# Hybrid decoder step: 32 sample tokens moved from the dense expert product to row gathers, gate values in two buffers

## The reference, cut to what matters

```
q  = standardize(x @ w_q)                 # 8 heads of 256
s1, s2 = scores of the two halves of q against 128 keys each
v1, i1 = top_k(s1, 16);  v2, i2 = top_k(s2, 16)
top_s, top_j = top_k(all 256 sums v1 + v2, 16)
expert = i1 * 128 + i2 of the chosen pairs   # one of 16384
gate   = softmax(top_s)
act = gelu(x . emb_u[expert]) * gate         # 8 x 16 = 128 experts a token
y   = sum of act * emb_v[expert]
```

## Time and profile before

| | us |
|---|---|
| median of 3 runs | 4821.25 |
| the profiled execution's own time | 4827.02 |
| its span, first to last instruction | 4825.2 |
| PE busy in the span | 4212.8 (87%) |
| DVE busy | 3123.2 (65%) |
| ACT busy | 1425.3 (30%) |
| POOL busy | 1019.4 (21%) |
| mean granted clock of PE | 0.938 of full |

### The profile page before, as it was taken

One profiled execution on the slowest core, in us unless ns is written; L12 is line 12 of the kernel. 1 busy time (PEld: TensorE's weight loads), 2 busy tenths in 40 slices (PEclk: granted clock), 3 DMA queues, 4 the chain that ended last, 5 costly groups with the idle time before them and its releaser, 6 DMA issues. The chain is left out here.

```text
span 4825.2 us, 61337 instructions
## 1 busy us (share of the span) xinstructions
PE 4212.8 (87%) x19753; PEld 3328.3 (69%) x19753; DVE 3123.2 (65%) x6997; ACT 1425.3 (30%) x2331; POOL 1019.4 (21%) x1145
## 2 busy tenths in 40 slices
PE   8999678667999999999588778898579999999995
PEld 1454334367999999999446522344569999999995
DVE  0144559996777777777545412489967777777776
ACT  0120013385323333332111100133672333333231
POOL 0000012294222222222100000112762222222221
PEclk9998799899999999999779988899899999999997
DMA  9777765535777777777377665655356777777773
GB/s 316 246 264 231 255 221 210 172 148 218 248 248 247 259 248 252 251 254 231 125 248 228 188 184 184 216 198 169 151 221 229 255 256 245 252 257 247 252 252 104
DMA packets 480396, 1083.53 MB, mean 225 GB/s; under 512 B 42782, under 2 KB 272175, under 8 KB 476672
## 3 DMA queue, kind: packets, MB, share of 16 engines
q1 hardware_dynamic: 289106, 680.98, 41.7%
q0 software_dynamic: 77392, 283.00, 18.0%
q10 hardware_dynamic: 113776, 118.10, 7.1%
HBM read 885.08 MB, written 196.83 MB: 224 GB/s over the span
## 5 line engine op out<-in xcount | busy, mean ns | idle before, releaser
L1494 PE MATMUL ps<-h_parts_d,u_parts_d 128*128 128x416 f32 x6144 | 1190.3, 353 | 26.6 <-ACT arena L1549 13.5
L1494 PEld LDWEIGHTS ps<-h_parts_d,u_parts_d 128*128 128x128 f32 x6144 | 1147.9, 188 | 59.0 <-ACT arena L1549 32.7
L1513 PE MATMUL ps<-a_parts_d,v_parts_d 128*128 128x416 f32 x4608 | 880.4, 351 | 4.3 <-DVE arena L1677 4.3
L1513 PEld LDWEIGHTS ps<-a_parts_d,v_parts_d 128*128 128x128 f32 x4608 | 861.3, 188 | 13.0 <-DVE arena L1677 5.7
L267 PE MATMUL ps<-ring,hT 128*128 128x512 f32 (+1 forms) x1440 | 637.2, 601 | 22.2 <-DMA ring<-in_gla_wo 12.1
L1544 ACT ACTIVATE v_parts_d<-ring 128x1024 fp32r<-128x1024 f32 x256 | 250.1, 1049 | 1034.6 <-PE ps L1513 1034.6
L1605 POOL DMA_INDIRECT arena<-in_peer_v,arena x256 | 240.9, 941 | 1432.6 <-DVE ps L1668 1430.2
L267 PEld LDWEIGHTS ps<-ring,hT 128*128 128x128 f32 (+1 forms) x1440 | 249.7, 177 | 379.4 <-issue 375.8
L1631 DVE TENSOR_TENSOR u_parts_d<-ring,u_parts_d 128x1024 fp32r<-128x1024 f32 x256 | 313.2, 1224 | 122.9 <-ACT u_parts_d L1542 122.9
L1605 POOL DMA_INDIRECT hT<-u_rows,arena x256 | 289.0, 1129 | 426.2 <-DVE hT L1652 375.0
L1542 ACT ACTIVATE u_parts_d<-ring 128x1024 fp32r<-128x1024 f32 x256 | 270.2, 1056 | 276.7 <-PE ps L1494 276.7
(11 more groups left out here) (269 smaller groups left out, 4380.7 us busy)
## 6 DMA issues: line engine op xcount, KB each, us to landing
ring<-in_peer_uT SPq DMA_DIRECT2D x256, 512.0 KB, 4.9
ring<-in_peer_v SPq DMA_DIRECT2D x256, 512.0 KB, 7.0
arena<-in_peer_uT SPq DMA_DIRECT2D x186, 512.0 KB, 5.5
u_rows<-arena SPq DMA_DIRECT2D x424, 128.0 KB, 4.0
gates_dense<-arena ACTq DMA_DIRECT2D x26, 2048.0 KB, 6.3
arena<-gates_dense ACTq DMA_DIRECT2D x64, 832.0 KB
ring<-in_ada_w SPq DMA_DIRECT2D x96, 512.0 KB, 4.7
u_rows<-arena SPq DMA_DIRECT2D x80, 512.0 KB, 6.3
```

The lines of the kernel that those rows point to most:

```text
L1494: mm = e.matmul(ps[:, tt % 2, 0:ND], w[:, m], hR[:, v, k], start=(k == 0 and n == 0), stop=(k == KC - 1 and n == 2))
L1513: mm = e.matmul(ps[:, 4 + m % 2, 0:ND], w[:, rows], aR[:, v, tt], start=begins, stop=ends)
```

## The change

The sample tokens leave the dense product: `ND` becomes 384. As 32 tokens of 128 experts each are as many rows as 128 partitions of 32, they are laid on all 128 partitions (four copies of the 32 tokens, two heads for each copy), and a turn gathers five rows (`ROWS`) where it gathered four. The fifth dot and the fifth accumulation stand at the end of `add_y`, the accumulation into `y_sample` in SBUF. In the search the sample tokens' queries of the four groups go to four quarters of one PSUM bank, behind the queries of each group's fourth tile, and are searched as one item: 17 items for 20. The gate table has 12 blocks. Two of the saved turns of `emb_u` go to the mixer's `stage_close`, four into the first four items of the search. The gates of a turn get two buffers, in the SBUF of `x`, which is kept in HBM meanwhile (`x_kept`) and loaded again behind the experts; the fifth rows of the gathers use it too. The loops of ACT and DVE hold two turns. ACT's `picked_gelu` stands later in its turn.

```
-DENSE = [(0, 0, 3 * P), (3 * P, SEQ, NS_TOK)]
-ND = 3 * P + NS_TOK
+ND = PICK * P
+ROWS = TPG + 1
+SPREAD = P // NS_TOK
-HEAD_TURNS, CLOSE_TURNS, IN_BUFS, OUT_BUFS = 70, 18, 2, 3
+HEAD_TURNS, CLOSE_TURNS, IN_BUFS, OUT_BUFS = 70, 20, 2, 3
...
# stage_close
-                    if w_o is not None and t < 4:
+                    if w_o is not None:
                         turner.turn(e, HEAD_TURNS + 2 * t + 10, HEAD_TURNS + 2 * t + 12)
...
+                if w_o is None:
+                    e.wait_ge(x_in, x_moved(l, 1))
...
-                        c = slice(DENSE[1][0], ND) if t > PICK else cols(t, np_)
+                        if t > PICK:
+                            for g in range(2):
+                                mm = e.matmul(ps[0:np_, 2 * (t % 4) + g, :], K["fold"], y_sample[:, g * 512:(g + 1) * 512], start=True, stop=True)
...
# stage_search
-            ITEMS = [(g, t, np_) for g in range(4) for t, np_ in TILES]
-            QBANKS = 3
-            turns_of = lambda n: range(VEC_TURNS + 2 * n, VEC_TURNS + 2 * n + 2)
+            ITEMS = [(g, t) for g in range(4) for t in range(4)] + [(3, 4)]
+            QBANKS, SAMPLE_BANK = 2, 2
+            turns_upto = lambda n: VEC_TURNS + 2 * n + min(n, 4)
+            turns_of = lambda n: range(turns_upto(n), turns_upto(n + 1))
...
                 def queries(n):
+                    g, t = ITEMS[n]
+                    if t > 3:
+                        return
                     if n >= QBANKS:
                         e.wait_ge(*qn_done(n - QBANKS + 1))
-                    q_rows.tile(e, n % NT, hT, n % QBANKS)
+                    q_rows.tile(e, t, hT, bank_of(n))
+                    if t == 3:
+                        q_rows.tile(e, 4, hT, SAMPLE_BANK, NS_TOK * g)
...
# stage_gates
-                body(NBLK // 2, 0)
...
+            def sp(e):
+                e.wait_ge(stage_over, 4 * here)
+                for i, np_ in TILES:
+                    e.dma_start(x_kept[i * P:i * P + np_], x[0:np_, i]).then_inc(x_in, 16)
...
# stage_experts
+            gt = [x.rearrange("p t c -> p (t c)")[:, v * DBLK * P:(v + 1) * DBLK * P].rearrange("p (b n) -> p b n", n=P) for v in range(2)]
+            u_got = [flat[:, j * D:(j + 1) * D] for j in range(TPG)] + [x[:, 3]]
+            v_got = [v_rows_buf[:, j] for j in range(TPG)] + [x[:, 4]]
...
# ACT, a turn
-                    if not first:
-                        picked_gelu(t - 1)
                     if not last:
                         e.wait_ge(*h_ps(t * TPG + 3))
                         hi_part(t + 1, 0)
...
                     a_hi(t, 2)
+                    if not first:
+                        picked_gelu(t - 1)
...
-                    if not last:
-                        gates(t + 1)
+                    if load:
+                        gates(t + 2, v)
...
# POOL, a turn
                     for j in range(TPG):
+                        if t:
+                            v_fetch(t - 1, j)
                     for j in range(TPG):
+                        u_fetch(t, j)
                     if t:
-                        v_fetch(t - 1)
-                    u_fetch(t)
+                        v_fetch(t - 1, TPG)
+                    u_fetch(t, TPG)
...
# DVE, add_y
+                    o = acc if j < TPG else y_sample
+                    e.scalar_tensor_tensor(out=o, in0=v_got[j], scalar=coef[:, j:j + 1], in1=o, op0=ALU.mult, op1=ALU.add
...
                         else:
                             dot(t, m - TPG)
+                    if not first:
+                        accumulate(t - 1, TPG)
+                    dot(t, TPG)
```

More of the change, by code:

```diff
@@ L257, in __init__, with tile @@
                 self.slots = {}
[L259 removed]
+            def tile(self, pe, t, src, bank, row=0):
                 np_ = TILES[t][1]
@@ L1587, in turn @@
                     a_hi(t, 3)
[L1588 to L1589 removed]
+                    if load:
+                        gates(t + 2, v)
                 e.sem_inc(h_read.sem, 2)
[L1592 to L1594 removed]
+                e.wait_ge(x_in, x_moved(l, 0))
+                gates(0, 0)
+                gates(1, 1)
+                o = spread.rearrange("p k (g n) -> p k g n", g=SPREAD)
+                e.activation(o, hT[:, :, SEQ:N].unsqueeze(2).broadcast_to([P, KC, SPREAD, NS_TOK]), ACT.Copy).then_inc(h_split.sem, 1)
+                e.activation(hR[:, 0], hT[:, :, 0:ND], ACT.Copy).then_inc(h_split.sem, 1)
                 hi_part(0, 0)
                 hi_part(0, 1)
[L1597 to L1600 removed]
+                turn(0, 0, first=True)
+                with e.Fori(0, turns // 2 - 2) as i:
+                    for u in (1, 2):
+                        turn(i * 2 + u, u % 2)
+                turn(turns - 3, 1)
+                turn(turns - 2, 0, load=False)
+                turn(turns - 1, 1, last=True, load=False)
                 picked_gelu(turns - 1)
@@ L1724, in dve @@
-                second_half(1)
-                with e.Fori(1, turns - 2) as t:
-                    first_half(t + 1)
-                    add_y(t)
-                    second_half(t + 1)
-                first_half(turns - 1)
+                for v in range(2):
+                    e.wait_ge(*xrow_ps(v + 1))
+                    b = 4 + 2 * v
+                    e.tensor_copy(xrow[:, v].rearrange("p (a k r) -> p k a r", a=4, k=KC),
+                                  ps[:, b:b + 2, :].rearrange("p b (k a r) -> p (b k) a r", a=4, r=STREAM)).then_inc(xrow_done.sem, 1)
@@ new lines, in dve @@
+                e.wait_ge(*xrow_done(2))
+                e.memset(Y[:, KEPT:].rearrange("p k n -> p (k n)"), 0.0).then_inc(zeroed.sem, 1)
+                e.memset(acc, 0.0).then_inc(zeroed.sem, 1)
+                e.memset(y_sample, 0.0).then_inc(zeroed.sem, 1)
+                e.wait_ge(*zeroed(3))
+                first_half(0, 0, 0)
+                second_half(0, 0)
+                first_half(1, 0, 1)
+                add_y(0, first=True)
+                second_half(1, 1)
+                with e.Fori(0, turns // 2 - 2) as i:
+                    for u in (1, 2):
+                        first_half(i * 2 + (u + 1), i + 1, (u + 1) % 2)
+                        add_y(i * 2 + u)
+                        second_half(i * 2 + (u + 1), (u + 1) % 2)
@@ L1730, in dve @@
+                first_half(turns - 2, turns // 2 - 1, 0)
+                add_y(turns - 3)
+                second_half(turns - 2, 0)
+                first_half(turns - 1, turns // 2 - 1, 1)
                 add_y(turns - 2)
-                second_half(turns - 1, last=True)
+                second_half(turns - 1, 1, last=True)
                 add_y(turns - 1)
@@ L1735, in dve @@
                 coefficients(turns - 1)
-                for j in range(TPG):
+                for j in range(ROWS):
                     accumulate(turns - 1, j)
```

344 lines of the change are left out of this document (175 added, 169 removed).

## The result

The changed kernel took 4863.36 us (median of 4 runs, 4856.74 to 4866.61) beside 4821.01 for the kernel before: a ratio of 1.0089, 95% interval 1.0071 to 1.0106. It is slower by 42 us where 54 less were forecast. Its profiled execution took 4860.7 us, with a span of 4858.9 and a mean granted clock of 0.915, where it was 0.938.

What follows compares the result with a forecast made beforehand. PE bounds the experts, DVE and PE nearly the search. Turns -15, gate buffers -6, experts' start and end +5, search -20, gates -24, mixers' close +6 sum to -54 us: 4767 us, range 4718 to 4810.

Steps and rivals of the forecast that it cites:

- Around the pause of 2.53 us in layer 0 it stayed at 1.00: Experts: PE's clock stayed at 2.4 GHz around one long pause in the earlier trace; used as evidence against rival B.
- rival B: Experts: the repeated pause makes PE's clock fall, 1.75 us in each of 62 turns, 4875 us; chance 8%.
- The pause: Experts: PE waits 2.7 us for the gelu in each turn instead of 0.24, from two added DVE instructions.
- The columns: Experts: 384 columns cost 174.5 ns a matmul for 187.8, 14.5 ns held fixed; 2.55 us less a turn.
- Rival C: Experts: the narrower matmul is no faster because weights set the pace; turn 38.2 us, 4882 us; chance 4%.
- Rival A: Experts: DVE's slack covers the added instructions, so a turn loses all of 2.55 us; 4629 us; chance 7%.
- Gates, gathers and gate buffers: Gates: one block fewer, -24 us; experts: nothing added for gathers, second gate buffer -6 us, both layers.
- The last pause of a layer: End of the experts: the last turn's pause of 2.53 us grows by 2.3 + 0.6 us.
- The search: Search: three items fewer for DVE, less PE losses: -10 us a layer, -20; from 0 to -37 a layer.
- the third turn of `emb_u`: Search, first four items: adds about 1.06 + 0.40 us each on PE; with the 6.3, some 10 us lost.
- Rival D: Search gains nothing or emb_u's third turn waits for loads, and turn gains nothing: 4802 us up; within forecast's range.
- The sample tokens' queries: Search: about 6.9 us more on PE once in four items, so DVE loses about 5.3 us in groups 2 to 4.

Runs made afterwards that it cites:

- e2_fill: The changed kernel with 14 more matmuls of 384 columns, results unused, in each turn behind hidden(t + 1, 3): 4781.47 us.
- e1_fifth_late: The changed kernel with the fifth accumulation and dot moved to the end of second_half, picked_gelu moved with them: 4659.63 us.
- e3_third_turn: The changed kernel with one of three emb_u turns moved into the middle of PE's queries in the first four search items: 4833.51 us.

## Why the prediction was wrong

- **The step that failed** is "Around the pause of 2.53 us in layer 0 it stayed at 1.00", with "I give the row of the experts more weight": from it the sum took the clock's loss at nothing, and rival B got 8%. That pause stands once in a layer, at its end. The same length in every turn is another case, and the earlier trace rows also showed the clock at 0.55 where PE works in short runs with waits between. The runs showed the clock at 0.53 behind the pause in every turn but the first ones: 82 us (e2_fill). B had the mechanism, at 1.75 us a turn and 4875 us; it is 1.3 us a turn. That the kernel's 4863 is so near 4875 is in part luck: some 28 us of it are the search's miss, below. The Trainium skill, TensorE: Matmul & The Clock Gate, section "A second HAM failure mode: psum-queue depth-cycling", describes a clock that swings between its two levels when PE idles often and shortly between groups of matmuls; this trace agrees, with 2.54 us of idle time in each turn of 37.54 us and a clock of 0.53 behind it.
- **The pause** was right: 2.7 us forecast, 2.54 measured, made by two instructions of 2.34 us, with the 0.55 us swallowed, as forecast.
- **The columns:** 14.5 ns a matmul were held fixed. 72 matmuls start in 1741.51 - 1729.03 = 12.48 us, 173.3 ns each, so everything shrank with the columns, and a turn without the clock's fall is 36.11 us for 36.32. Rival C is out. Rival A's cover was not there, as argued; e1_fifth_late shows that the place decided it.
- **Gates, gathers and gate buffers** came nearly as forecast: -10.4 and -11.2 us a layer for -12, no wait for a gathered row, and no wait for gates. The last pause of a layer is 4.85 us for some 5.4, but behind it the 24 matmuls of line 1547 take 6.39 us where those of a turn take 4.32: there too the clock's fall (0.50 in the 3.4 us behind it) was left out.
- **The search:** the third turn of `emb_u` was costed at its busy time, 1.06 + 0.40 us. Its load is the term that was left out: 3 us of wait an item, and 1.7 us of slower queries behind most of these waits. The forecast of -10 us a layer became +4; e3_third_turn puts it at -13 to -15 (-17 to -19 against the changed kernel). Rival D had named that wait, "the third turn of `emb_u` waits for its loads", but it was priced only as a gain that fails. The sample tokens' queries were right: a step of 17.29 us once in four items, 5.1 us over 12.2, for some 5.3.
- **The sum without the clock** would have been right in sign: e2_fill's 4781 us lies inside the forecast's range of 4718 to 4810. That it is only 14 us over 4767 hides two misses that go against each other: the search, 28 us worse than forecast, and the turn, 60 x 0.21 = 13 us better. The ends of the range are themselves 3 to 5 us off: 54 us below 4767 and 40 us above it are 4713 and 4807.

## What to carry to other kernels

An engine's instruction costs what it costs at its place: the same two instructions cost 204 us more ahead of the `a_lo` that PE's next matmuls wait for than behind it, so before adding work look for the place where that engine already waits. A pause that repeats in every turn is to be priced with the clock that may fall behind it, and a pause seen once says nothing of it. Where a step gets a third transfer, ask when its buffer comes free, not how long its instructions are busy.

## What the runs showed that was not expected

- Unused matmuls can pay: 14 of them a turn won 82 us. Four of them won 7 us in the one run, as the end of the pause is set by the gelu and the clock still fell in most turns.
- In the changed kernel the clock held in the first turn of a layer with the full pause (36.11 us), and fell in each turn after it, behind the same pause. Pauses of 0.53 and 1.39 us a turn left it at 1.00 throughout, 1.84 did so in few turns, 2.54 in the first one alone.
- Between these two widths a matmul's pace followed its columns, with weights loaded for each: 187.8 ns at 416 and 173.3 at 384 are both 0.451 ns a column. No run here shows these matmuls at another width.
